# Regrouping weight places, evictions and mix products of a two-block model kernel on one core

## Time and profile before

| what | us |
|---|---|
| runs | 976.75, 981.56, 981.55 |
| median | 981.55 |
| the profiled execution | 984.01 |
| its span | 982.3 |
| TensorE busy | 910.4 (93%) |
| weight loads of TensorE busy | 728.4 (74%) |
| VectorE busy | 406.7 (41%) |
| ScalarE busy | 261.7 (27%) |
| GpSimd busy | 66.3 (7%) |
| chain: TensorE, SP's queue, DMA | 80%, 10%, 4% |
| HBM read | 227.54 MB |

### The profile page before, as it was taken

One profiled execution on the slowest core, in us unless ns is written; L12 is line 12 of the kernel. 1 busy time (PEld: TensorE's weight loads), 2 busy tenths in 40 slices (PEclk: granted clock), 3 DMA queues, 4 the chain that ended last, 5 costly groups with the idle time before them and its releaser, 6 DMA issues.

```text
span 982.3 us, 13560 instructions
## 1 busy us (share of the span) xinstructions
PE 910.4 (93%) x5310; PEld 728.4 (74%) x5310; DVE 406.7 (41%) x906; ACT 261.7 (27%) x588; POOL 66.3 (7%) x88
## 2 busy tenths in 40 slices
PE   8979899999999976676899999999999999999997
PEld 7848688888766543343888887888888888878886
DVE  4275767655323111013432560734134246164422
ACT  2234523103211210112245152212112714312201
POOL 5152200012000000002000000000000000000011
PEclk9989999999999988898899999999999999999999
DMA  9915976599999999999353433323435343432311
GB/s 344 405 64 219 368 299 261 214 426 421 360 421 420 421 420 421 421 422 408 49 199 132 169 136 121 129 86 129 148 110 191 133 169 135 165 92 104 125 45 44
DMA packets 35124, 229.52 MB, mean 234 GB/s; under 512 B 5984, under 2 KB 6016, under 8 KB 8176
## 3 DMA queue, kind: packets, MB, share of 16 engines
q1 hardware_dynamic: 30944, 222.05, 58.3%
q0 software_dynamic: 1312, 4.71, 1.4%
q10 hardware_dynamic: 2800, 1.85, 0.6%
HBM read 227.54 MB, written 1.06 MB: 233 GB/s over the span
## 4 chain that ended last, share of the span: by engine, by line
PE 80%; SPq 10%; DMA 4%; DVE 3%; issue 1%; ACT 1%; POOL 0%; DVEq 0%; ACTq 0%; POOLq 0%
PE bank L425 28%; PE bank L1026 11%; SPq L1051 9%; PE bank L889 6%; PE bank L867 6%; PE bank L731 3%; PE bank L632 3%; DMA s<-in_w_down 3%; PE bank L909 3%; PE bank L703 2%; PE bank L746 2%; PE bank L463 2%; PE bank L990 1%; PE bank L924 1%; PE bank L417 1%
## 5 line engine op out<-in xcount | busy, mean ns | idle before, releaser
L425 PE MATMUL bank<-hT,ring 128*128 128x256 f32 x1152 | 255.7, 381 | 4.5 <-DMA ring<-in_first_pieces 4.3
L425 PEld LDWEIGHTS bank<-hT,ring 128*128 128x128 f32 x1152 | 218.3, 191 | 37.0 <-DMA ring<-in_first_pieces 4.7
L1026 PE MATMUL bank<-ring,s 128*128 128x256 f32 x512 | 111.2, 379 | 0.0
L1026 PEld LDWEIGHTS bank<-ring,s 128*128 128x128 f32 x512 | 97.1, 190 | 13.1
L1723 DVE SCALAR_TENSOR_TENSOR z<-z,bank 128x256 f32<-128x256 f32 x9 | 3.8, 422 | 151.3 <-ACT z L1273 151.3
L731 PE MATMUL bank<-s,z 128*32 128x256 f32 (+1 forms) x448 | 46.2, 424 | 16.5 <-DMA ring<-in_w_up 4.5
L889 PE MATMUL bank<-ring,hT 128*128 128x256 f32 x256 | 56.4, 380 | 0.0
L867 PE MATMUL bank<-hT,ring 128*128 128x256 f32 x256 | 55.6, 379 | 0.0
L731 PE MATMUL bank<-ring,z 128*32 128x256 f32 (+1 forms) x336 | 40.8, 438 | 15.9 <-DMA hT<-in_w_up 6.2
L889 PEld LDWEIGHTS bank<-ring,hT 128*128 128x128 f32 x256 | 48.3, 190 | 7.3 <-issue 0.9
L867 PEld LDWEIGHTS bank<-hT,ring 128*128 128x128 f32 x256 | 48.5, 190 | 6.5
(11 more groups left out here) (395 smaller groups left out, 1366.2 us busy)
## 6 DMA issues: line engine op xcount, KB each, us to landing
ring<-in_layer_pieces SPq DMA_DIRECT2D x64, 1024.0 KB, 4.8
ring<-in_first_pieces SPq DMA_DIRECT2D x49, 1024.0 KB, 8.3
s<-in_w_gate SPq DMA_DIRECT2D x15, 1024.0 KB, 18.4
s<-in_w_down SPq DMA_DIRECT2D x14, 1024.0 KB, 27.0
s<-in_w_up SPq DMA_DIRECT2D x13, 1024.0 KB, 14.3
ring<-in_w_up SPq DMA_DIRECT2D x11, 1024.0 KB, 21.1
ring<-in_w_gate SPq DMA_DIRECT2D x10, 1024.0 KB, 23.9
ring<-in_w_down SPq DMA_DIRECT2D x9, 1024.0 KB, 23.8
```

The costliest lines, as they stand in the source:

```text
L425: mm = pe.matmul(b[:, 0:T], w[:, (k0 + kb) * CW + m * P:(k0 + kb) * CW + (m + 1) * P], rhs[:, kb, :], start=(kb == 0), stop=(kb == nk - 1))
L1026: mm = pe.matmul(xo[j, tt][:, 0:CW], yT[:, kb, tt * P:(tt + 1) * P], w[:, kb, :], start=(kh == 0 and kb == 0), stop=(kh == 1 and kb == KB ...
```

## The change

- ScalarE's exp for the softplus moves from in front of the K evictions to behind the V evictions.
- `ADA_LAG` becomes 0, and the last call of `ada_job`, in the gates, goes.
- A 14th buffer `ws` of 1 MB makes a 20th expert place, fourth in `moe_slots`; `onesr`, `sel4` and `rdiag` lie in it and are built (the first two by GpSimd) behind the expert stage instead of at the opening; `tri` moves into `rxp`.
- Ten expert pieces are loaded early, the first four behind loads 20, 22, 24, 26 instead of three behind 14, 18, 22.
- In the units the mix of u - 1 goes between gate and up products, the gather of u + 1 goes in front of the turn; ScalarE and VectorE follow that order.

```
-ADA_LAG = 1
+ADA_LAG = 0
-EARLY_LOADS = (14, 18, 22, 41, 42, 43, 44, 45, 48)
+EARLY_LOADS = (20, 22, 24, 26, 41, 42, 43, 44, 45, 48)
...
-        tri = sb("tri", [P, P])
+        tri = rxp[:, 512:512 + P]
-        onesr = sb("onesr", [MLH, P])
-        sel4 = sb("sel4", [MLH, MLH, P])
+        ws_t = sb("ws", [P, 2048])
+        sel4 = ws_t[0:MLH, 0:MLH * P].rearrange("p (h t) -> p h t", h=MLH)
+        onesr = ws_t[0:MLH, 512:512 + P]
-        rdiag = sb("rdiag", [P, TT, P])
+        rdiag = ws_t[:, 768:768 + TT * P].rearrange("p (t c) -> p t c", t=TT)
...
-            [wg_t[:, :], hT[:, :, :].rearrange("p b t -> p (b t)"), rxp[:, 0:KB * CW]]
-        moe_slots = [RING + i for i in (7, 8, 6, 0, 2, 3, 1, 4, 5, 10)] + [(NB1 + i) % RING for i in range(RING)] + \
-            [RING + i for i in (9, 11, 12)]
+            [wg_t[:, :], ws_t[:, :], hT[:, :, :].rearrange("p b t -> p (b t)"), rxp[:, 0:KB * CW]]
+        moe_slots = [RING + i for i in (7, 8, 6, 11, 0, 2, 3, 1, 4, 5, 10)] + [(NB1 + i) % RING for i in range(RING)] + \
+            [RING + i for i in (9, 12, 13)]
...
                 for c, done in ((0, S["gate_done"]), (1, S["gu_done"])):
+                    if c == 1 and u >= 1:
+                        mix(u - 1)
...
                         reorder_in()
-                        gather(1)
-                        turn(0)
-                        down_own(0)
-                        reorder_out()
-                        continue
-                    mix(u - 1)
-                    turn(u)
                     if u + 1 < NU:
                         gather(u + 1)
+                    turn(u)
                     down_own(u)
+                    if u == 0:
+                        reorder_out()
...
-            act.wait_ge(S["sp_wanted"], 1)
-            step(f(labs, labs, ACT.Exp, scale=-1.0), S["sp_ready"])
             for m in range(4):
                 out_copy(kvT[:, m, :], T)
             for tt in range(TT):
                 out_copy(vnat[:, tt, :], 512)
+            act.wait_ge(S["sp_wanted"], 1)
+            step(f(labs, labs, ACT.Exp, scale=-1.0), S["sp_ready"])
...
                     out_copy(t[:, m, :], T, ACT.Tanh, scale=0.5)
-                    if m == 1 and t is tga:
-                        ada_job()
...
                     weights_turned(0)
-                    gathered(1)
+                if u + 1 < NU:
+                    gathered(u + 1)
                 act.wait_ge(S["heT_done"], u + 1)
...
-                if 0 < u < NU - 1:
-                    gathered(u + 1)
...
                 for u in range(NU):
+                    if u >= 1:
+                        mix_add(u - 1)
                     act_own(u)
...
-                    if u >= 1:
-                        mix_add(u - 1)
...
-            step(g.memset(onesr[:, :], 1.0))
...
-            step(g.memset(sel4[:, :, :], 0.0))
-            step(g.affine_select(out=sel4[:, :, :], in_=sel4[:, :, :], compare_op=ALU.not_equal, fill=1.0, base=0,
-                                 pattern=[[-1, MLH], [0, P]], channel_multiplier=1))
...
+            g.wait_ge(*chunk_free[max(E0 + m for m in range(3 * EXPERTS) if slot[E0 + m] == RING + 11)])
+            step(g.memset(onesr[:, :], 1.0))
+            step(g.memset(sel4[:, :, :], 0.0))
+            step(g.affine_select(out=sel4[:, :, :], in_=sel4[:, :, :], compare_op=ALU.not_equal, fill=1.0, base=0,
+                                 pattern=[[-1, MLH], [0, P]], channel_multiplier=1))
             step(g.memset(rxv[:, :, 0:PAD], 0.0))
```

More of the change, by code:

```diff
@@ L336, in build @@
         C = Banks(psum[4:6], sem("c_done"), sem("c_free"))
-        slot_full = [sem(f"slot_full{i}") for i in range(RING + 13)]
+        slot_full = [sem(f"slot_full{i}") for i in range(RING + 14)]
         chunk_used = sem("chunk_used")
@@ L1062, in _ @@
                         RING + 9: ((S["xg_raw"], 4 * TT),), RING + 10: ((B.done, B.upto("yb7")), (S["vln_ready"], 1)),
-                        RING + 11: ((S["router_done"], 5),),
-                        RING + 12: ((S["ada_summed"], ADA_POOL), (S["ada_summed_v"], ADA_CHUNKS - ADA_POOL),
+                        RING + 12: ((S["router_done"], 5),),
+                        RING + 13: ((S["ada_summed"], ADA_POOL), (S["ada_summed_v"], ADA_CHUNKS - ADA_POOL),
                                     (B.free, B.upto("gm3")))}
```

## The result

| | before | changed kernel |
|---|---|---|
| median of the runs of this comparison | 980.91 | 968.17 (967.23 to 969.3, 4 runs) |
| ratio | | 0.9879, 95% interval 0.9848 to 0.9911 |
| the profiled execution | 984.01 | 967.23 |
| its span | 982.3 | 965.5 |
| TensorE busy | 910.4 | 900.9 |

The changed kernel is 1.2% faster; 968.0 was forecast. A second series gave 967.99 (967.23 to 969.04, 6 runs), ratio 0.9854 (0.9823 to 0.9886). One execution of early_back (1353 us) and three of the kernel before in the later series (1349, 1895 and 2405 us) ran far slower than all others and are left out of every median and ratio.

The account below looks back on a forecast made before the run. Before the router TensorE sets the pace, with three holes; after it a full DMA queue of expert loads does. Terms -16.0 - 0.5 + 2.5 + 0.3 = -13.7 gave 968 us, range 960 to 976.

Parts of the forecast that it names:

- Softplus, 7.05 and 1.85: Value products: start 7.05 us earlier once K evictions skip the softplus wait, and run 1.85 shorter at full clock.
- The lag, 0.85 + 4.26 + 1.95: Modulation pieces summed at once: holes before second v piece (0.85) and first gate piece (4.26) go; gate products 1.95 shorter.
- The whole front: Everything up to the first scores: softplus and lag terms together, 16.0 us earlier.
- slower: Rival: ScalarE waits for GpSimd at its sixth and seventh jobs, delaying v and gate evictions; +9.8, 991 us; chance 0.04.
- VectorE's margin of 0.3: First transposes: probabilities ready at 103.4, TensorE wanting them at 103.7, so no wait, by 0.3 us.
- its top-k ends at 80.8 as now: VectorE's top-k in the front: said to end at 80.8 us, unchanged from before.
- Later early pieces cost nothing: Front's DMA queue: four early expert pieces behind load 20 and on cost 2.5 us transfers at share 0.71: nothing.
- VectorE late: Rival: one more 4.5 us block leaves TensorE waiting 4.2 at the first transposes; -9.5, 972 us; chance 0.18.
- Twentieth place, -0.5: Expert stage: second sorted piece is loaded with the first; bounds 0 and 1.6 us gained, -0.5 taken.
- Mix order, +2.5: Last unit's tail: down products lose clock after idle time; bounds 0 and 7.5 us, +2.5 taken.
- Constants, +0.3: Root chain behind the expert stage: GpSimd's rebuilding runs beside it; bounds 0 and 1.3 us, +0.3 taken.

Follow-up runs that it names:

- early_back: Changed kernel with its first early expert pieces moved back behind loads 14, 18, 22, 24; 972.71 us, ratio 0.9931.
- softplus_only: Kernel before with only the softplus exp moved behind the V evictions; 971.64 us, ratio 0.9902.
- order_only: Kernel before with only the units' new order (mix between gate and up, gather before turn); 983.12 us, ratio 1.0016.
- places_only: Kernel before with only the twentieth place, the later early pieces and the constants built behind the experts; 979.98 us, ratio 0.9992.
- front_both: Kernel before with softplus exp moved and modulation sums without lag, early pieces still behind loads 14, 18, 22; 970.03 us, ratio 0.9880.
- no_place: Changed kernel without the twentieth place, three early pieces behind 20, 22, 24, constants built at the opening; 966.98 us, ratio 0.9865.
- front_late_pieces: Kernel before with softplus exp moved, sums without lag and three early pieces behind loads 20, 22, 24; 966.36 us, ratio 0.9867.
- front_late_warm: front_late_pieces with 22 products of ones behind the last mix; 967.88 us, ratio 0.9876.

## Why the prediction was right, and where not

**Softplus, 7.05 and 1.85: right.** V moved by 8.35, of which 1.4 came from the opening, so 6.95; its products went from 3.71 to 1.88. softplus_only shows the same alone. That the clock would come back with TensorE at work was forecast from the rows and stands in them now, 1.00 from 60 to 94 us. By the rule of the Trainium skill (TensorE: Matmul & The Clock Gate, What's actually happening), that the throttled state is the default and activity releases it, the traces agree: 3.71 us for the products behind the wait of 6.77, 1.88 without it.

**The lag, 0.85 + 4.26 + 1.95: right, its size in part by luck.** Both holes are gone in the changed kernel, and the gate products went from 8.86 to 7.07, 1.79 for 1.95. The whole front moved by 17.5 at the first scores, 16.1 without the opening; 16.0 was forecast. I had read the 4.26 and the 1.95 from one execution; order_only, with the same front, has 3.42 and nothing of the 1.95, so measured from that execution the front gains about 3 us less. None of ScalarE's new waits for GpSimd came, so the rival "slower" had no ground. ScalarE's last sum there began at 89.39, after the last multiply's end. GpSimd's timeline of the changed kernel:

```profile
57.14 18.38 POOL L2033 TENSOR_TENSOR ring<-ring,rxp 128x2048 f32<-128x2048 f32 x4 [23.65 <-DVE s L1501]
77.66 9.16 POOL L2033 TENSOR_TENSOR ring<-ring,rxp 128x2048 f32<-128x2048 f32 x2 [2.14 <-DMA ring<-in_first_pieces]
```

Four multiplies are done by 75.5 and the last two by 86.8, near the 87.9 of my working.

**VectorE's margin of 0.3: wrong sign, small.** VectorE's timeline of the changed kernel:

```profile
71.03 4.57 DVE L1514 TENSOR_SCALAR s<-s 128x128 f32<-128x128 f32 x1
...
83.50 3.47 DVE L1513 TENSOR_SCALAR s<-s 128x256 f32<-128x256 f32 x1
87.01 0.29 DVE L1514 TENSOR_SCALAR s<-s 128x256 f32<-128x256 f32 x1
...
102.24 0.35 DVE L1553 TENSOR_SCALAR tmp<-tmp,rt 128x256 f32<-128x256 f32 x1
```

The second mask (83.50) is held until the last multiply ends at 86.8, as I had counted the blocks, but behind it the rest of the mask and all of log1p, 3.7 us together, run in the open where I had put 3.0, and the scores' normalisation follows them. The probabilities were done at 102.59; TensorE was free at 102.22. The first mask's second half (71.03) is held in the same way, until the fourth multiply ends at 75.5. Before, no fourth multiply stood there:

```profile
72.38 0.23 DVE L1518 TENSOR_SCALAR s<-s 128x128 f32<-128x128 f32 x1
```

So "its top-k ends at 80.8 as now" was wrong: it ended at 83.50, though all before it ran 1.4 earlier. By the rows it cost nothing, since the second mask has to wait for the last multiply in any case, and that I had not worked out.

**"Later early pieces cost nothing": the step that failed.** I looked only for what the pieces would cost in their new place, at a DMA share of 0.71, and not for what they would cost in their old one once the front is faster. There, behind load 14, a piece delays the landing of load 15, GpSimd's last two multiplies start 2.4 to 2.6 us later, the mask's second half is held until the later end of the last one, TensorE waits 1.9 to 2.0 us longer at the first transposes and runs 3.4 us at half clock behind that, 1.7 more. So this part is worth 3.6 to 3.7 us with the front changed; without it the runs can't tell its worth from nothing (places_only). The total came out right since I had taken the front as if nothing delayed it, which is true only with this part in place. My rival "VectorE late", at 972, is the mechanism that front_both (970.0) and early_back (972.7) show, but its terms were others: a wait of 2 us longer and not 4.2, and the 1.7 of clock that it did not have.

**Twentieth place, -0.5: not seen.** The second sorted piece is issued 1.2 us behind the first (237.24 and 238.44) in place of 1.63, so the place does what it says. But from the read of `order` to the last landing nothing moved that the spread of 201.6 to 202.75 would show, and no_place is by its runs not slower than the changed kernel. No run shows the 0.5.

**Mix order, +2.5: measured +1.7.** The half clock came as forecast, at 5.33 for 3.64 (5.03 to 6.12 over five profiled executions in this order). My first row for it, 1.75 lost of 5.30, was the right one; I had gone higher, to 2.5, by the products behind 6.46 us of idle time, and the mix behind, which I let be slow at the far end of the bounds, took 3.70 us.

**Constants, +0.3: right.** VectorE's timeline in the root chain:

```profile
452.42 0.52 DVE L1797 TENSOR_SCALAR small<-rt 128x2 f32<-128x2 f32 x1
...
453.20 0.51 DVE L1802 SCALAR_TENSOR_TENSOR small<-small 128x2 f32<-128x2 f32 x1
```

GpSimd's at the same time:

```profile
452.40 0.51 POOL L2064 MEMSET ws<- 4x512 f32 x1
453.06 0.63 POOL L2065 TENSOR_SCALAR_AFFINE_SELECT ws<-ws 4x512 f32<-4x512 f32 x1
```

These two operations took 0.17 and 0.16 before, and now 0.52 and 0.51, each until the GpSimd instruction beside it ended. From the last mix's end to the scaling products it is 6.79 us for 6.45 before: +0.34. Only the second hold is in the open; the first passes while VectorE would wait for ScalarE anyway (`small` L1801 follows it by 0.59 us, 0.57 before). Over all runs it is 6.5 to 6.8 us in the six executions with rebuilt constants and 6.2 to 6.45 in the seven others without the products of ones.

**The sum.** -16.1 (front) + 0.5 (transposes) + 1.7 + 0.3 = -13.6, within 0.1 of the forecast sum, with its parts off by up to 0.8. The rest of the profiled difference, 16.8 - 13.6 = 3.2, is the opening's 1.4, the layers' 1.65, 0.35 between `order` and the last landing (202.35 for 202.70) and 0.92 at the scaling products (5.51 to the first layer for 6.43), less 1.1 in the gather in front of `order`, which ran at half clock (5.44 for 3.81). By medians the change is worth 12.7 and 14.7 us in the two series, 13.7 between them. So close a hit is luck in part: the 0.5 at the transposes and the 0.5 that the place did not bring make up for the 0.8 that the tail cost less, and the front was measured against an execution that other executions of the same code differ from by up to 3 us.

## What to carry to other kernels

When a front is made faster, ask of every transfer that used to sit harmlessly in it whom it now holds up: here a part of the change whose worth alone the runs can't tell from nothing is worth 3.6 to 3.7 us beside the others. A wait that appears on TensorE costs its length and can cost a stretch at half clock behind it: 1.7 us more behind the waits of 2.3 and 2.5 us here. And a change that comes out as forecast can still hold parts that cost: the front with the later pieces alone (966.4) does as well as all of it (968.2), within the spread, with far fewer edits.

## What the runs showed of the hardware that was not expected

- On VectorE the small TENSOR_SCALAR, 0.29 us by itself, took up to 4.57 us beside a GpSimd multiply of 128x2048, ending with it; MAX8 and MATCH_REPLACE8 in the same stretch (75.6 to 83.5) took 0.43 and 0.41 throughout, with a multiply beside them from 77.66 on. The Trainium skill (SBUF — State Buffer, SBUF: two separate sides) says that the side which starts first holds the shared ports for its whole instruction; the holds agree with it. That MAX8 and MATCH_REPLACE8 pass beside a multiply is told here by the rows alone.
- Between two multiplies back to back one such operation gets through: in front_both L1515 ends at 87.70, with the first multiply of the pair, and L1516 is then held for the whole second one.
- A GpSimd MEMSET of 4x512 and a select of 0.63 us hold two-column VectorE operations in the same way.
- Where the stretches at half clock fall differs between executions of the same code: 1.00 and 0.90 over the first 17 us in two executions of the changed kernel; 3.81 and 5.44 us for the gather in front of `order` in front_late_pieces and front_late_warm, whose programs are alike up to the tail; 7.17 and 8.86 us for the first gate products in order_only and before. Each of these moves a run by 1 to 2 us.
- Behind 44 records of products of ones TensorE began its next products 2.63 us after all that they wait for was there. The cause is open, the step out of a branch among the rivals.
